# A hybrid pooling and windowed-attention block on eight cores: the opening re-ordered, so that short transfers, both first tiles' projections and the first attention visits come earlier

## The reference

```python
h_ctx = modulate(rms_norm(ctx, norm_pre_g), c_shift, c_scale)   # adaLN: silu(cond) @ w_mod + b_mod
k_ctx, v_ctx = h_ctx @ w_in[K columns], h_ctx @ w_in[V columns]
h = modulate(rms_norm(x, norm_pre_g), shift, scale)
xa, ga, q, k, v, gb, gm = split_columns(h @ w_in)               # 1024 -> 5632 columns
y_a = pool_mixer(xa, pool_w, pool_scale) * silu(ga)             # windows 2/4/8/16 over 4 groups of 128
y_b = windowed_attention(rope(q), rope(k), v, k_ctx, v_ctx, sink) * silu(gb)   # +-128 tokens + context
g = sigmoid(gm)
merged = g[:, :1024] * (y_a @ w_branch_a) + g[:, 1024:] * (y_b @ w_branch_b)
out = x + gate * rms_norm(merged @ w_out, norm_post_g)
```

## Time and profile before

| | |
|---|---|
| median of 3 runs | 2260.73 us (2259.37 to 2319.16) |
| the profiled execution | 2259.51 us |
| its span, slowest core (core 4) | 2257.9 us; the cores lie between 2255.9 and 2257.9 |
| TensorE (PE) busy | 2186.2 us, 97% of the span |
| VectorE (DVE) / ScalarE (ACT) / GpSimd (POOL) busy | 66% / 51% / 34% |
| mean granted TensorE clock | 0.984 to 0.988 |

### The profile page before, as it was taken

How to read it: one execution, slowest core, us unless ns; L and a number is a source line. 1 busy time by engine, 2 the same in 40 slices (tenths; PEclk the granted TensorE clock), 3 DMA queues, 4 the chain that set the end, 5 groups by cost and what they waited for, 6 DMA issues and landing times.

```text
span 2257.9 us, 67485 instructions; the slowest of 8 cores (2255.9 to 2257.9 us)
## 1 busy us (share of the span) xinstructions
PE 2186.2 (97%) x24216; PEld 1331.3 (59%) x24216; DVE 1492.1 (66%) x4226; ACT 1144.8 (51%) x2341; POOL 759.8 (34%) x983
## 2 busy tenths in 40 slices
PE   3689999999999999999999999999999999999998
PEld 2565566566556656556656556665655655655664
DVE  0456676776676767667677667666666766766765
ACT  1346445555545555544554554555554455455453
POOL 0233333333233233333333323323333333332332
PEclk7799999999999999999999999999999999999999
DMA  9991332332232232333234233223233323323312
GB/s 247 232 182 48 79 81 68 77 90 72 71 83 72 74 81 75 73 78 81 68 78 99 72 68 87 72 74 81 74 73 80 80 69 77 88 71 68 81 46 66
DMA packets 234453, 194.04 MB, mean 86 GB/s; under 512 B 197504, under 2 KB 205840, under 8 KB 231568
## 3 DMA queue, kind: packets, MB, share of 16 engines
q1 hardware_dynamic: 231680, 168.68, 29.9%
q0 software_dynamic: 2448, 21.04, 4.9%
HBM read 125.25 MB, written 33.56 MB: 70 GB/s over the span
## 4 chain that ended last, share of the span: by engine, by line
PE 94%; DMA 3%; ACT 1%; DVE 1%; issue 0%; POOL 0%; another core or an unknown queue 0%; SPq 0%; DVEq 0%; POOLq 0%; ACTq 0%
PE pb L580 32%; PE pb L587 23%; PE pb L875 10%; PE pb L933 10%; PE pb L772 7%; PE pb L829 7%; PE pb L867 5%; DMA s_PT<-x 2%; DMA s_ropet<-rope 1%; PE pb L533 0%; PE pb L359 0%; ACT s_xsb L501 0%; ACT s_xsb L489 0%; POOL s_kTp L651 0%
## 5 line engine op out<-in xcount | busy, mean ns | idle before, releaser
L580 PE MATMUL pb<-s_W,s_hT 128*128 128x512 bf16 (+1 forms) x3584 | 772.1, 364 | 0.0
L801 ACT ACTIVATE s_PT<-pb 128x512 bf16<-128x512 f32 x1024 | 528.2, 604 | 122.6 <-PE pb L772 122.1
L587 PEld LDWEIGHTS pb<-s_hT,s_W 128*128 128x128 bf16 x9216 | 525.1, 98 | 81.8 <-issue 66.9
L587 PE MATMUL pb<-s_hT,s_W 128*128 128x128 bf16 x9216 | 563.5, 220 | 0.2 <-issue 0.2
L580 PEld LDWEIGHTS pb<-s_W,s_hT 128*128 128x128 bf16 x3584 | 338.2, 98 | 309.4 <-issue 1.9
L856 ACT ACTIVATE s_Tm<-pb 128x512 bf16<-128x512 f32 x256 | 152.9, 597 | 381.9 <-PE pb L580 368.8
L811 DVE TENSOR_TENSOR s_PT<-s_PT,s_maskb 128x512 bf16<-128x512 bf16 (+1 forms) x384 | 191.8, 513 | 90.9 <-ACT s_PT L796 45.8
L879 POOL TENSOR_TENSOR s_mg<-s_ub,s_scr 128x512 bf16<-128x512 f32 x128 | 161.9, 1265 | 245.4 <-DVE s_scr L860 245.2
L875 PE MATMUL pb<-s_wmf,s_ybT 128*128 128x512 bf16 x1024 | 242.6, 380 | 0.0
L838 DVE SCALAR_TENSOR_TENSOR s_yb<-pb,s_small,s_Gb 128x64 bf16<-128x64 f32 x1024 | 220.1, 277 | 28.2 <-DVE s_small L835 1.1
L933 PE MATMUL pb<-s_wmf,s_mgT 128*128 128x512 bf16 x1008 | 227.8, 379 | 0.0
(11 more groups left out here) (126 smaller groups left out, 2659.6 us busy)
## 6 DMA issues: line engine op xcount, KB each, us to landing
s_xr<-x SPq DMA_DIRECT2D x63, 512.0 KB, 4.6
y<-s_xr SPq DMA_DIRECT2D x63, 512.0 KB, 3.0
s_xt<-x SPq DMA_DIRECT2D x62, 512.0 KB, 4.3
s_W<-w_in POOLq DMA_DIRECT2D x10, 1024.0 KB, 32.9
s_ropet<-rope SPq DMA_DIRECT2D x64, 128.0 KB, 2.0
s_wmf<-w_mod SPq DMA_DIRECT2D x2, 2048.0 KB, 12.9
s_W<-w_mod SPq DMA_DIRECT2D x2, 2048.0 KB, 28.0
s_wmf<-w_mod POOLq DMA_DIRECT2D x2, 2048.0 KB, 18.5
```

Of the source, the lines that this page charges most:

```text
L580: E("pe", lambda e, k=k: e.matmul(out=pb[:, c0:c0 + n], lhsT=h[:, k, :], rhs=W[:, wblk, k, c0:c0 + n], start=(k == 0), stop=(k == 7)), rea ...
L587: E("pe", lambda e, c=c, k=k: e.matmul(out=pb[:, c * 128:(c + 1) * 128], lhsT=W[:, wblk, k, c * 128:(c + 1) * 128], rhs=h[:, k, :], start= ...
L801: E("act", lambda e, g=g: e.activation(out=PT[:, jb, g, :], in_=banks[g][0][:, :], func=AF.Exp, scale=0.125), reads=[banks[g][1]], writes= ...
```

## The change

It moves instructions and adds none of weight. In the SP queue the four short transfers (`bmodT`, `gpreT`, `sinkb`, `edge`) go behind conditioning block 0, the context tiles go ahead of block 2, and block 3 goes behind latent tiles 0 and 1, the pooling parameters and rope table 0. The rope tables of tiles 1 and 2 get buffers of their own in the still unused `mgT`. The mask's cast load goes to the head of POOL's queue. In the opening both first tiles are projected, and all five visits of period 0 are made, before and between the gate blocks; period 0 no longer has them. `weights_c` comes after the norm of the fourth context tile and the first gate block. In period 1 the merge gate of block 10 and its `B_mm` come after `ga` and the first `gb`; for the first three tiles the transposes of `yb` stand behind that. In `finish()` the transposes of the last tile's `mg` are drawn ahead between the output products, and `out_stat` comes before the last multiply by the gain.

```diff
         ld(cT, cT_d, "cT")
         load_wmod(0, "sp")
+        ld(bmodT, bmodT_d, "bmodT")
+        ld(gpreT, gpreT_d, "gpreT")
+        ld(sinkb, sink_d.partition_broadcast(128), "sinkb")
+        ld(view(edge, 0, [[1, 64]]), edge_d, "edge")
         load_wmod(1, "sp")
-        ld(bmodT, bmodT_d, "bmodT")
-        load_wmod(2, "sp")
...
         def weights_a():
+            load_cast(view(maskb, 0, [[1, 256]]), mask_d, "maskb")
             load_w(0, reads=[bf("W7")])
...
+        def rope_of(t):
+            if t in (1, 2):
+                return AP(mgf.tensor, mgf.offset + (t - 1) * 256, [list(mgf.ap[0]), [128, 2], [1, 128]]), bf(f"rope{t}")
+            return ropet[:], bf("ropet")
...
             u = A_mm(tm0, 1)
             B_mm(tm1, 1, u)
-            so = [out_mm(t - 1, 0), out_mm(t - 1, 1)]
+            turn_mg_half(0)
+            so = [out_mm(t - 1, 0)]
+            po = out_pe(1, mgT, None)
+            turn_mg_half(1)
+            out_sq(1, *po)
+            so.append(out_gain(1, *po))
             out_stat(t - 1)
-            turn_mg_half(0)
+            last = hT[TT % NH], f"hT{TT % NH}"
+            so2 = [out_mm(t, 0, *last)]
             out_evac(t - 1, so)
-            turn_mg_half(1)
-            so = [out_mm(t, nb, hT[TT % NH], f"hT{TT % NH}") for nb in range(2)]
+            po = out_pe(1, *last)
+            out_sq(1, *po)
             out_stat(t)
-            last_evac(t, so)
+            so2.append(out_gain(1, *po))
+            last_evac(t, so2)
...
-            if hasG:
+            if hasG and p > 1:
                 tm = gm(p - 1, 10)
...
             if hasP:
                 gb(p + 1, 0)
+            if p == 1:
+                tm = gm(p - 1, 10)
+                B_mm(tm, 1, u)
+            if hasA and p < FRONT:
+                do_ybT(p)
...
         start_loads()
-        load_wmod(3, "sp")
-        ld(gpreT, gpreT_d, "gpreT")
+        load_wmod(2, "sp")
         for i in range(2):
             load_staged(i, x_d[0, i * 128:(i + 1) * 128, :])
...
         load_rope(0)
-        ld(sinkb, sink_d.partition_broadcast(128), "sinkb")
-        ld(view(edge, 0, [[1, 64]]), edge_d, "edge")
+        load_wmod(3, "sp")
+        load_rope(1)
+        load_rope(2)
...
         weights_b()
+        make_wp()
+        g3 = mod_mm(3)
+        turn_front(hT[1][:], [f"hT1_{k}" for k in range(8)])
+        mod_row(3, *g3)
         mod_fin(3)
         mod_end()
...
         ctx_kv(0, 1)
-        turn_front(hT[1][:], [f"hT1_{k}" for k in range(8)])
+        fold_pool()
         norm_mod(hT[0], "hT0", 0)
-        fold_pool()
         P_kv(0)
+        P_xa(0)
+        norm_mod(hT[1], "hT1", 0)
+        q = P_q(0)
+        next(q)
+        P_xa(1)
+        next(q)
+        next_load()
+        next_load()
+        visit(0, 0)
+        P_kv(1)
+        V_edges(0)
+        visit(0, 1)
+        q = P_q(1)
+        next(q)
+        visit(0, 2)
+        mask(0, 2)
         norm_front(staged(2))
-        P_xa(0)
         turn_ctx(0)
         mod_ctx(0)
+        next(q)
+        visit(0, 3)
+        mask(0, 3)
+        ctx_kv(1, 0)
+        visit(0, 4)
+        gate_block(0)
         norm_front(staged(3))
...
+        weights_c()
+        gate_block(1)
         ctx_kv(1, 1)
```

65 lines of the change are left out of this document (32 added, 33 removed).

## The result

The changed kernel takes 2267.14 us (median of 7 runs, 2265.45 to 2270.95), the kernel before 2260.73 (median of its 7 runs): a ratio of 1.0034, 95% interval 1.0024 to 1.0045. That is within 2%, as forecast, but it is 6.4 us slower where 1.7 us faster had been forecast, and lies above the range of 2251 to 2266.

The account below looks back on a forecast made before the run. Steady periods were taken as pure PE work and the opening as waiting for loads, with W9's landing limiting the gain. out_mm(0) +0.9 and the end -1.5 gave -0.6 on 2259.51: 2258.9, forecast 2259 us, range 2251 to 2266.

Parts of the forecast that it names:

- part 3: From weights_c to out_mm(0): W9 lands at 152.5, out_mm(0) starts at 176.8 against 175.85, +0.9 us.
- The restart: POOL's queue after running dry: weights_c issued at 106.6, packets again at 111.2 after 4.6 of starting up, 5.1 us without weights.
- SP's earlier loads: Loads of gg, rope 3, tile 5 and the residual come earlier in SP's queue, delaying W9 by 1.5 to 2 us.
- The casts' own pace: Weight blocks on POOL's queue from W6 to W9: 6.6 us per 2 MB block, taken as unchanged.
- 20.7 + 1.7 + 1.9: From W9's landing to out_mm(0): 20.7 us solid PE work, 1.7 for half clock, 1.9 for the mg wait.
- The wait for mg: Period 1, PE before the transposes of mg: waits for DVE's product and POOL's sum, +1.9 us.
- The clock: PE's granted clock halves after the wait for W9, now falling behind gm(0, 9): +1.7 us.
- The end: finish(): PE's gap of 0.96 closes and out_stat no longer waits for the gain product, -0.6; together -1.5 us.
- each us behind that is a us of the whole time: Opening: each us that block 3 lands after about 51 adds a us to the total.
- rival B: Slower: pool_w and rope 0 fall behind W0, block 3 lands at 60, 2269; rope alone 54, 2263; chance 0.23 together.
- Rival A: POOL's queue never runs dry: W9 lands at 147 to 147.6, total 2250.2 to 2253.8; chance 0.30.
- Rival C: Early projections stay where they were, held by ACT or DVE; only the end's -1.5 remains, 2258; chance 0.47 shared with forecast.

Follow-up runs that it names:

- experiment 1: Changed kernel with the loads of W7 and W8 moved from weights_c to the end of weights_b: 2261.87 us, ratio 0.9981 to the kernel before.
- experiment 3: Kernel before with weights_c and weights_d issued late, behind P_kv(1) in period 0: 2274.37 us, ratio 1.0036.
- experiment 4: Kernel before with the rope tables of tiles 1 and 2 staged early in mgT's columns: 2262.36 us, ratio 0.9997.
- experiment 7: Kernel before with only the changed finish(): 2262.66 us, ratio 0.9997.
- experiment 11: Changed kernel with W7, W8 early, gm(0, 9) late, block 3 heading POOL's queue, pool_scale and pool_w before the latent tiles, make_wp later: 2262.49 us, ratio 0.9986.
- experiment 5: Changed kernel with gm(0, 9) and its A_mm behind the attention products of tile 1 in period 1: 2269.39 us, ratio 1.0043.
- experiment 6: Changed kernel with both W7 and W8 loaded early and gm(0, 9) behind tile 1's attention products: 2263.07 us, ratio 1.0018.
- experiment 8: Changed kernel with W7 and W8 loaded early and period 1 in the order of the kernel before: 2261.37 us, ratio 0.9992.

## Why the prediction was wrong

**The step that failed** is the middle of part 3, "W9 lands at 145.6 + 5.1, and 1.5 to 2 later still ... 152.5". On the slowest core W9 landed at 157.2, and this one term is 4.7 of the 5.7 us by which out_mm(0) was missed (176.8 forecast, 182.51). Its mechanism, the queue that runs dry because `weights_c` is late, was right, and experiments 1 and 3 show it by removing and by making it. What failed is the size of one term, which the prediction put at nothing: the pace of the casts behind the gap. Term by term:

- *The restart* was forecast at 111.2 and came at 110.7, but by two errors that cancel. `weights_c` came at 109.4 instead of 106.6 (block 3 in use at 51.6 instead of 50, and 57.8 us from there instead of 56.6). The queue then needed 1.3 us to begin, not 4.6. The Trainium skill ("DMA: Bandwidth & Descriptors", section Specifications) gives about 1 us for the first byte of a POOL-issued transfer, and the prediction set it aside for the row of W0. Here five cores come near it with 1.3 us, core 3 among them; cores 0, 4 and 7 needed 2.4 to 2.7, core 1 of experiment 3 needed 2.5. The 4.6 of the earlier trace rows was measured with SP's queue full, and didn't carry over to an idle one.
- *SP's earlier loads* were put at 1.5 to 2 and measured 2.0.
- *The casts' own pace* was taken as unchanged, 6.6 us a block, and took 5.0 us more of queue time. That is the whole miss of W9. One part can be read: when W9's last packet had landed, 0.3 MB more had been moved than before (6.59 MB against 6.31), which is 1.6 us at 6.31 MB in 37.0. The rest, some 3 us, is a lower rate, 0.157 instead of 0.171 MB for each us of queue time. Kernels whose queue never ran dry were slow in part as well (experiment 4, core 3: 6.39 MB in the last 43.2 us before W9). And the same opening, run in another session, took up to 42.3 us for the six blocks (experiment 7). So why the rate was lower here stays open, and part of it may be the session's.

**Behind W9** the prediction had 20.7 + 1.7 + 1.9 = 24.3 us, and it took 25.3. The wait for mg was 1.68, as said. The clock cost more than 1.7: gm(0, 9) took 3.57 instead of 1.89 and A_mm 1.91 instead of 1.03, 2.6 for these two alone. The longer wait isn't the reason. PE worked at half clock for 5.5 us here (0.50 from 157.3 to 162.8) and for 5.8 us behind the 4.33 us of before, where the prediction read only the first 4; the clock column still says 0.50 in the next stretch of that trace (core 4):

```profile
146.00:147.50 1.50, 1.50 (x9) 0.84 (x8) 0.00 (x0) 0.60 (x1) 0.00 (x0) 0.50 1.01 227
```

**The end** was forecast at -1.5 and gave -0.6. PE's gap of 0.96 closed, but "DVE's two out_evac steps (1.5) fit into PE's last 1.7 us" is false. They began at 2257.74, behind a gain that waits for ACT's square, and the statistics of the last tile, now behind them, could start at 2259.06 only.

**One core for eight.** The whole sum was made on one core, and before that did no harm, since the cores lay within 2 us. In the new kernel the slowest core is a draw from a wider spread. The mean span of all cores in seven executions is 2260.4, the slowest's median 2265.6, 5.2 above it; in the profiled execution before the slowest was 0.8 above the mean (2257.9, 2257.1), in the later sessions 1.6 to 2.1. By these numbers I estimate that of the 6.4 us some 3 are a later mean, and some 3.5 the spread. The prediction's rule, "each us behind that is a us of the whole time", holds (experiment 11). Its rival B at 54 and 60 us for block 3 is what the latest core met in experiments 1, 5, 6 and 8 (53.9 to 59.2), while the earliest stood at 48.9 to 50.1, my value.

**Rival A** was priced too well. With the queue kept full (experiment 1) it was to give 5.7 to 9.3 us, and gave 1.2 by the medians (3.1 on the mean core, 4.3 by the ratio). Its W9 was 147 to 147.6, measured 147.7 to 154.2. And the new order has a longer way from the first projection to out_mm(0): 114 to 115 us in experiment 11, where no load is waited for, before 106.1 to 108.3. PE's busy time in it is the same (92.6 to 95.4 us, before 92.4 to 94.0); what grew is PE's waiting, above all for ACT, which norms the second sample's context tiles between the exponentials of the visits (experiment 11, core 5; the changed kernel has the same wait, 6.18 on core 3):

```profile
104.11 1.01 PE L549 MATMUL pb<-s_ident,s_xsb 128*128 128x128 bf16 x8 [6.19 <-ACT s_xsb L517]
```

The longer way gives back 7 to 9 of the 9.5 us that the first projection gained from one profiled execution to the other (67.57 to 58.09), so there was little to win even with every load on time. **Rival C** is excluded: the first projection did move, to 54.5 to 58.1. **What held:** first projection at 56 (58.1 on core 3), the dip in the DMA share behind 106, the waits named, the solid rest, and no change by over 2%.
